# Layer 1's second memory-value group computed in layer 0's last norm, and that norm's modulation row summed by VectorE in layer 1's first feed forward

## The chip, the cores and the metric

The program runs on one core of one Trainium2 chip. The core has five engines that run their own instruction streams: TensorE (PE) for matmuls, VectorE (DVE) and ScalarE (ACT) for elementwise work, GpSimd (POOL), which here mostly issues gathers, and SyncE (SP), which here issues the weight loads. They meet only through semaphores. The metric is the device time of one execution in microseconds (us).

## What is computed

Two blocks run one after the other. The first (`first_block`) has two layers; each is a SwiGLU feed forward and a norm, a mixer (conv, recurrence, pooling) and a norm, cross attention to a memory `mem` and a norm, a second feed forward and a norm. The second block has two layers of attention and a product-key expert lookup (`peer_block`), modulated by rows that come from a condition vector. Cut to what the change touches:

```python
# first block, layer l
h = layer_norm(ALPHA * h + 0.5 * swiglu(h, ffn1_gate[l], ffn1_up[l], ffn1_down[l]), ln_g[l, 0], ln_b[l, 0])
z = h @ w_in[l]                                        # mixer input, 24 chunks of weights
...
h = layer_norm(ALPHA * h + mix, ln_g[l, 1], ln_b[l, 1])
v = (mem @ wv).reshape(bsz, m, CA_HEADS, CA_HEAD_DIM)   # depends on mem alone, not on h
o = jnp.einsum('bhsm,bmhd->bshd', p, v)                 # p: softmax of q k
h = layer_norm(ALPHA * h + cross_attn(...), ln_g[l, 2], ln_b[l, 2])
h = layer_norm(ALPHA * h + 0.5 * swiglu(h, ffn2_gate[l], ...), ln_g[l, 3], ln_b[l, 3])
# second block, layer i
mod = jax.nn.silu(c) @ ada_w[i] + ada_b[i]              # a "modulation row" is 512 of its 6144 columns
```

The activations `x` and `mem` have 256 tokens of 1024 features. Keys and values of the memory and the modulation rows depend on nothing that the first block computes, so they can be computed anywhere before their use.

## The kernel before, in words

Weights come in chunks of 512 KB. SP loads them in the order in which it is written, into two places. The feed forward's weights go into `fw`, two buffers for each of gate, up and down (`ff_loads`, L527 is the issue): the load of a tile waits until PE has used the tile two before it (`ff_done`). All other weights go through `wring`, four slots of one chunk (`load`, L510): each load waits until four chunks back has been used (`chunk_done`, one count that PE and DVE add to). SP issues in program order, so a load that stands behind another also starts behind it.

A feed forward is 22 tiles. For each, PE does 16 matmuls of gate and up (`gate_up`, L1529) and 8 of down (`down`, L1537), in the order gate_up(q+1), down(q). ACT makes the silu, DVE multiplies it with up (`hidden_tile`, L3148), and down(q) waits for that. DVE fills its time with expert work of the second block's context: per slot a gather of 512 KB by POOL (L712) into a ring of 8 (`rows`), and one instruction on DVE: a dot product (L2780) or a weighted sum (L2789). DVE does 8 of these (`HEAD_SLOTS`) behind hidden_tile(0), then 4 behind each hidden tile, in a loop of five turns of four tiles.

After a feed forward, PE, DVE and ACT pass the norm's work to and fro (`layer_norm`: residual L3249, mean L1568, centring L3258, squares on ACT, mean of squares L1568 again, reciprocal L3267, scaling L3271, x_t by ACT L1762). PE fills the waits with work that is given to it as `between`: in a layer's first norm the values of memory head 0 (`value_between`, L1592), in the second keys (`key_between`), in the third and fourth a modulation row (`mod_row_between`, which calls `mod_row_part`, L856: 8 matmuls of 512 columns). Further modulation rows are summed on DVE near the end of each feed forward (`mod_row_sums`, L3176 and L3179: 8 instructions over 512 columns, into `row_acc`), and PE only adds up the partitions with one matmul (L1560). ACT takes each row out of PSUM (`mod_row_take`, L1762) into the one buffer `mod_row` and writes it out by a small DMA (L1808), and waits at the next take until that DMA has landed.

In the mixer PE runs groups of two chunks (`group`; L787 and L796) and between them the levels of the recurrence (`level`, L1642), which DVE takes (`take_level`, L3358 and L3356). Behind level 8 stands group 13, memory head 1's values into `ca_v[:, 1]`, in both layers, and then PE waits for DVE's take of levels 7 and 8.

A matmul of 128x256 stands in the trace as two records, so "x32" is 16 matmuls.

Of the kernel before, what the change touches and what calls it, by code (L numbers as in the profile page):

```python
# [21 lines left out]
ALU = mybir.AluOpType  # L22
ACT = mybir.ActivationFunctionType
AX = mybir.AxisListType.X

P = 128
# [27 lines left out]
MIX_CHUNKS = 60  # L54
ADA_CHUNKS, QKV_CHUNKS, WO_CHUNKS, PQ_CHUNKS = 48, 12, 8, 16
# [156 lines left out]
def program(nc, a, out):  # L212

    with ExitStack() as ctx:
# [242 lines left out]
        row_acc = view(arena, 6656, 512)  # L457
        mod_tm = view(mem_tile, 7 * T, P)
# [28 lines left out]
        NORM_BANK = 3  # L487
# [16 lines left out]
        def _(eng):  # L504
# [37 lines left out]
            def mod_row_loads(i):  # L542
                chunk_loads(a["second_w"], LAYER_1 + WR * ROW_AT[i], WR)
# [17 lines left out]
            for l in range(L):  # L561
                mix_at, row_at = l * MIX_CHUNKS, CTX_MOD_ROWS + 4 * l
                for w in range(2):
# [3 lines left out]
                    if w == 0:  # L567
                        mod_row_loads(row_at)
# [4 lines left out]
                    with sp.loop(FT_TURNS, **ff_turn) as i:  # L573
# [3 lines left out]
                    if w == 0:  # L577
# [178 lines left out]
        def _(eng):  # L756
# [762 lines left out]
            def feed_forward(h_ready):  # L1519
# [25 lines left out]
                mod_row_free()  # L1545
                gate_up(1)
# [9 lines left out]
                pe.skip(chunk_done, WR)  # L1556
                for arrived in weights_in:
                    pe.skip(arrived, 16)
                eng.wait_ge(chunk_done, pe.now(chunk_done))
                mm(ps_d[0:2, :], mean_d[:, 0:2], row_acc, start=True, stop=True).then_inc(  # L1560
# [26 lines left out]
            def value_between(i0, i1):  # L1587
                for i in range(i0, i1):
                    b, k = i // KT, i % KT
                    if b == 0 and k % 4 == 0:  # L1590
                        chunk(k // 4)
                    ins = mm(ps_b[:, b * T:(b + 1) * T], mem_t[:, k, b * P:(b + 1) * P],  # L1592
# [25 lines left out]
            for l in range(L):  # L1618
                feed_forward(h_take if l else h_have)
                layer_norm(value_between)  # L1620

                def group(g, c, src, ready=None, tm=False, between=None):
                    eng.wait_ge(z_done, pe.now(z_done, 1))
                    odd = (g + 1 if g < 12 else g) % 2
                    bank = ps_b[:, odd * 512:(odd + 1) * 512]
                    if tm:
# [25 lines left out]
                group(13, 26, mem_t, tm=True)  # L1652
# [83 lines left out]
                layer_norm(mod_row_between, finish if l == L - 1 else None)  # L1736
# [21 lines left out]
        def _(eng):  # L1758
# [33 lines left out]
            def mod_row_take(i, bank, row):  # L1792

                if bank == 2:
# [1830 lines left out]
```

## Time and profile before

| | us |
|---|---|
| median of 3 runs | 3248.68 |
| lowest and highest | 3248.24, 3252.84 |
| the profiled execution | 3234.46 |
| its span on the core | 3232.2 |
| PE busy in the span | 3055.6 (95%) |
| DVE, ACT, POOL busy | 2133.4, 952.0, 1226.2 |
| layer 0's last norm (from the last down matmul to layer 1's first feed forward) | 964.66 to 976.20 |
| layer 1's first feed forward, on PE | 976.20 to 1206.09 |
| layer 1's first norm and mixer | 1206.09 to about 1370 |

Times inside the trace are from the span's start. A row of the timeline is: start, duration, engine, line, operation, how many records, and in brackets the idle time ahead of it with its releaser. PE's matmuls overlap by a little, so a stretch is best read from start to start.

### The profile page before, as it was taken

What the parts mean: (1) busy time and instruction counts of PE and PEld (TensorE: products, weight loads), DVE (VectorE), ACT (ScalarE), POOL (GpSimd) and SP (SyncE); (2) the same over time, 40 slices, a digit from 0 to 9 for tenths busy, and PEclk for the clock granted to TensorE, in tenths of its full rate; (3) what the DMA queues carried; (4) which work ended last, traced back from release to release, by engine and by line L of the source; (5) the groups of instructions that cost most, each with busy time, mean ns of one, the idle gap of its engine ahead of it and who ended that gap; (6) DMA issues with size and microseconds to landing.
All of it is one profiled execution on the core that took longest, in us unless ns stands there. A gap on an engine that the chain in (4) does not pass through costs nothing.

```text
span 3232.2 us, 39640 instructions
## 1 busy us (share of the span) xinstructions
PE 3055.6 (95%) x13179; PEld 2183.1 (68%) x13185; DVE 2133.4 (66%) x4328; ACT 952.0 (29%) x2504; POOL 1226.2 (38%) x1136
## 2 busy tenths in 40 slices
PE   9999999999999999999999999989888999987777
PEld 7688888888888888887885845535335855532224
DVE  7877889756555457766455695667555596577444
ACT  2320012211001002121003464335455464343333
POOL 1003545344435443343430254434443144444332
PEclk9999999999999999999999999999999999999999
DMA  9787989798998997788988899999999899999998
GB/s 363 256 288 281 373 352 350 267 359 330 355 353 347 356 330 272 268 338 344 354 308 294 336 422 419 421 419 421 418 421 378 319 420 420 421 421 421 421 421 352
DMA packets 252469, 1164.47 MB, mean 360 GB/s; under 512 B 27304, under 2 KB 34952, under 8 KB 186400
## 3 DMA queue, kind: packets, MB, share of 16 engines
q0 software_dynamic: 153792, 828.44, 63.6%
q1 hardware_dynamic: 98480, 334.10, 28.5%
q8 instruction: 80, 1.31, 0.2%
q14 instruction: 69, 0.57, 0.0%
q10 hardware_dynamic: 48, 0.05, 0.0%
HBM read 1161.39 MB, written 1.10 MB: 360 GB/s over the span
## 4 chain that ended last, share of the span: by engine, by line
PE 32%; DMA 16%; DVE 5%; ACT 4%; issue 1%; POOL 0%; ACTq 0%; SPq 0%; POOLq 0%; DVEq 0%
DMA ring<-in_peer_uv,idx 12%; PE ps_a L1471 12%; PE ps_b L1529 5%; DMA arena<-in_peer_uv,idx 3%; PE ps_a L1537 2%; DVE ring L2962 2%; ACT arena L1762 2%; PE ps_a L774 1%; PE ps_b L1292 1%; PE ps_b L1237 1%; PE ps_b L787 1%; ACT L1762 1%; PE ps_a L1292 1%; PE ps_b L1028 1%; ACT wts L1762 1%
## 5 line engine op out<-in xcount | busy, mean ns | idle before, releaser
L1471 PE MATMUL ps_a<-ring,arena 128*128 128x512 f32 x1728 | 819.4, 608 | 129.1 <-ACT arena L1762 128.6
L749 POOL DMA_INDIRECT ring<-in_peer_uv,idx x448 | 494.8, 1104 | 879.0 <-PE ps_a L1471 620.8
L2962 DVE SCALAR_TENSOR_TENSOR ring<-ring,h_tm 128x1024 f32<-128x1024 f32 x448 | 546.7, 1223 | 378.0 <-DMA ring<-in_peer_uv,idx 377.3
L712 POOL DMA_INDIRECT ring<-in_peer_uv,idx_now x512 | 580.7, 1134 | 415.3 <-DVE arena L2780 151.4
L1471 PEld LDWEIGHTS ps_a<-ring,arena 128*128 128x128 f32 x1728 | 308.1, 191 | 561.3 <-ACT arena L1762 293.8
L1529 PE MATMUL ps_b<-x_t,ring 128*128 128x256 f32 x2816 | 623.3, 380 | 0.8 <-DMA ring<-in_ffn 0.5
L1529 PEld LDWEIGHTS ps_b<-x_t,ring 128*128 128x128 f32 x2816 | 533.6, 190 | 79.0 <-ACT x_t L1762 3.5
L1762 ACT ACTIVATE arena<-ps_b 128x256 f32<-128x256 f32 (+3 forms) x218 | 99.3, 457 | 1195.9 <-PE ps_b L1529 827.7
L1537 PE MATMUL ps_a<-arena,ring 128*128 128x256 f32 x1408 | 318.7, 380 | 0.0
L2780 DVE SCALAR_TENSOR_TENSOR arena<-ring,h_tm 128x1024 f32<-128x1024 f32 x256 | 299.1, 1220 | 20.0 <-DMA ring<-in_peer_uv,idx_now 16.6
L1537 PEld LDWEIGHTS ps_a<-arena,ring 128*128 128x128 f32 x1408 | 267.7, 190 | 39.1 <-issue 3.5
L1762 ACT ACTIVATE wts<-dots 128x1 f32<-128x1 f32 (+1 forms) x514 | 103.8, 202 | 621.2 <-DVE ring L2962 529.1
L3148 DVE SCALAR_TENSOR_TENSOR arena<-ps_b,arena 128x256 f32<-128x256 f32 x88 | 37.3, 424 | 331.0 <-PE ps_b L1529 189.6
L1762 ACT ACTIVATE arena<-consts,wts 128x128 f32<-128x128 f32 x512 | 205.5, 401 | 52.9 <-PE ps_a L1471 5.0
L2789 DVE SCALAR_TENSOR_TENSOR arena<-ring,stage,arena 128x1024 f32<-128x1024 f32 x160 | 195.1, 1278 | 5.7 <-DMA ring<-in_peer_uv,idx_now 5.6
L787 PE MATMUL ps_b<-x_t,wring 128*128 128x256 f32 x896 | 197.8, 381 | 0.3
L787 PEld LDWEIGHTS ps_b<-x_t,wring 128*128 128x128 f32 x896 | 167.0, 190 | 27.6 <-ACT x_t L1762 4.6
L774 PE MATMUL ps_a<-arena,wring 128*128 128x256 f32 (+1 forms) x896 | 169.5, 350 | 3.1 <-ACT arena L1762 1.9
L774 PEld LDWEIGHTS ps_a<-arena,wring 128*128 128x128 f32 x896 | 150.6, 191 | 22.0 <-ACT arena L1762 2.7
L1762 ACT ACTIVATE wts<-wts,gates 128x1 f32<-128x1 f32 x512 | 150.7, 294 | 16.6
L2789 DVE SCALAR_TENSOR_TENSOR arena<-ring,wts,arena 128x1024 f32<-128x1024 f32 x92 | 114.9, 1288 | 50.6 <-DMA ring<-in_peer_uv,idx_now 50.4
L1762 ACT ACT_TABLE_LOAD x105 | 134.7, 1283 | 12.0 <-PE ps_b L1529 8.7
(460 smaller groups left out, 3357.9 us busy)
## 6 DMA issues: line engine op xcount, KB each, us to landing
ring<-in_ffn SPq DMA_DIRECT2D x264, 512.0 KB, 7.0
wring<-in_second_w SPq DMA_DIRECT2D x166, 512.0 KB, 4.8
wring<-in_mix_w SPq DMA_DIRECT2D x120, 512.0 KB, 6.4
ring<-in_ada_rows POOLq DMA_DIRECT2D x44, 512.0 KB, 5.7
ring<-in_second_w SPq DMA_DIRECT2D x12, 1024.0 KB, 10.2
ring<-in_peer_uv,idx_now POOLq DMA_INDIRECT x512, 8.4
ring<-in_peer_uv,idx POOLq DMA_INDIRECT x448, 14.8
arena<-in_second_w SPq DMA_DIRECT2D x13, 512.0 KB, 11.1
```

The lines of the kernel that those rows point to most:

```text
L712: G.indirect_dma_start(rows[:, s, :], None, table, bass.IndirectOffsetOnAxis(ap=idx_now[:, half, s:s + 1], axis=0)).then_inc(rows_in[s], p ...
L749: G.indirect_dma_start(pairs[slot].rearrange("p c d -> p (c d)"), None, a["peer_uv"], bass.IndirectOffsetOnAxis(ap=idx[:, b, s:s + 1], axi ...
L774: ins = mm(acc_t[:, j, cols], w[:, k * P:(k + 1) * P], src[:, k, cols], start=i == 0, stop=i == KT - 1)
L787: ins = mm(bank[:, t * T:(t + 1) * T], w[:, k * P:(k + 1) * P], src[:, k, :], start=k == 0, stop=k == KT - 1)
L1292: ins = mm(out, part_of(place, k), src[:, k, :], start=k == 0, stop=k == KT - 1)
L1471: ins = mm(ps_a[:, b * D + j * 512:b * D + (j + 1) * 512], diags[:, at % DIAGS, :], pairs[at % PAIRS][:, 1, j * 512:(j + 1) * 512], start= ...
L1529: ins = mm(bank[:, part * T:(part + 1) * T], fw[:, ft % 2, part, k * P:(k + 1) * P], x_t[:, k, :], start=k == 0, stop=k == KT - 1)
L1537: ins = mm(acc_t[:, j, :], fw[:, ft % 2, 2, j * P:(j + 1) * P], hidden[:, ft % 2, :], start=opens and j % 2 == 0, stop=last, skip_group_ch ...
L1762: return nc.scalar.activation(out, in_, func, **k)
L2780: V.scalar_tensor_tensor(acc[s % 2], rows[:, s, :], 1.0, h, ALU.mult, ALU.mult, accum_out=out).then_inc(row_used, ve.adds(row_used))
L2789: ins = V.scalar_tensor_tensor(acc[s % 2], rows[:, s, :], w, acc[s % 2], ALU.mult, ALU.add)
L2962: V.scalar_tensor_tensor(row, row, 1.0, h_tm[:, n // SLOTS, :], ALU.mult, ALU.mult, accum_out=dots[:, n % SLOTS:n % SLOTS + 1]).then_inc(d ...
```

## The change

Four things change. (1) Layer 0's last norm gets `moved_between` in place of `mod_row_between`: 16 matmuls that compute layer 1's head 1 values (chunks 26 and 27 of layer 1's mixer weights, constant `MOVED`) into PSUM bank 1; ACT evicts them to `moved_v`, a place of its own. (2) In layer 1's mixer group 13 is gone; the chunks and slots behind the first two move by two, and layer 1's first norm takes its values from slots 2 and 3. (3) The modulation row that stood in the norm (row index 6) is summed by DVE in layer 1's first feed forward, behind the 8 head slots and ahead of the loop, into `row_acc_2`; PE gets one more matmul at that feed forward's end, into `ps_c`, and ACT one more take there. (4) SP's loads follow: two chunks instead of four ahead of layer 1's feed forward, row 6's four chunks where row 7's stood, and row 7's four chunks between the fourth and the fifth turn of that feed forward's loop of loads.

```diff
+MOVED = 26
+        row_acc_2 = view(arena, 7168, 512)
+        moved_v = view(extra, 2 * D, NB, T)
...
                     if w == 0:
-                        mod_row_loads(row_at)
+                        mod_row_loads(row_at - l, 2 * l)
...
-                    with sp.loop(FT_TURNS, **ff_turn) as i:
+                    looped = FT_TURNS - 1 if (l, w) == (1, 0) else FT_TURNS
+                    with sp.loop(looped, **ff_turn) as i:
...
+                    elif (l, w) == (1, 0):
+                        mod_row_loads(row_at, 2)
+                        for ft in range(FT_STEP):
+                            for part in range(3):
+                                ff_loads(looped * FT_STEP + (l * (2 * FT) + (w * FT + 2 + ft)), ft, part)
+                        chunk_loads(a["mix_w"], mix_at, 2, 2)
+                        chunk_loads(a["mix_w"], mix_at + 2, MOVED - 2)
+                        chunk_loads(a["mix_w"], mix_at + MOVED + 2, MIX_CHUNKS - WR - MOVED - 2)
+                    elif l == 0:
+                        chunk_loads(a["mix_w"], MIX_CHUNKS + MOVED, 2)
...
                 gate_up(0, True)
                 mod_row_free()
+                if second_row:
+                    eng.wait_ge(z_done, pe.now(z_done))
                 gate_up(1)
...
+                if second_row:
+                    mm(ps_c[0:2, :], mean_d[:, 0:2], row_acc_2, start=True, stop=True).then_inc(
+                        row_summed, pe.adds(row_summed))
+                    pe.skip(mod_row_taken, 1)
                 mm(ps_d[0:2, :], mean_d[:, 0:2], row_acc, start=True, stop=True).then_inc(
...
                 between(0, 1)
+                if between == value_between and l:
+                    eng.wait_ge(mod_row_taken, pe.now(mod_row_taken, 1))
...
+            def moved_between(i0, i1):
+                if i0 == 0:
+                    mod_row_free()
+                for i in range(i0, i1):
+                    b, k = i // KT, i % KT
                     if b == 0 and k % 4 == 0:
                         chunk(k // 4)
+                    ins = mm(ps_b[:, 512 + b * T:512 + (b + 1) * T], mem_t[:, k, b * P:(b + 1) * P],
                              wring[:, k // 4, (k % 4) * T:(k % 4 + 1) * T], start=k == 0, stop=k == KT - 1)
...
-                group(13, 26, mem_t, tm=True)
+                if l == 0:
+                    group(13, MOVED, mem_t, tm=True)
...
-                                v = (ca_v0, ca_v[:, 1], early_v[l], ca_v[:, 3])[h][:, m, :]
+                                v = (ca_v0, moved_v if l else ca_v[:, 1], early_v[l], ca_v[:, 3])[h][:, m, :]
...
-                layer_norm(mod_row_between, finish if l == L - 1 else None)
+                layer_norm(mod_row_between if l else moved_between, finish if l == L - 1 else None)
...
                 feed_forward()
+                if l:
+                    mod_row_take(row_at - 1, SECOND_ROW, mod_row)
                 mod_row_take(row_at, 2, mod_row)
...
                 hidden_tile(0)
                 some_slots(summing, h, at, HEAD_SLOTS, acc_first)
+                if (l, w) == (1, 0):
+                    mod_row_sums(l, w, row_acc_2, 1)
                 with ve.loop(FT_TURNS, up_done=FT_STEP, silu_done=FT_STEP, down_done=FT_STEP, hidden_done=FT_STEP,
```

How the order of instructions moves, at the three places that matter. PE in layer 1's mixer, around level 8, before (L787 a group, L1642 levels, L796 the value group, L1658 to L1660 what needs the taken levels):

```order
212 L787 MATMUL ps_b<-x_t,wring 128x256 x16
213 L1642 MATMUL ps_a<-arena 128x128 x12
214 L796 MATMUL ps_b<-wring,mem_t 128x256 x16
215 L1658 MATMUL ps_a<-arena 128x128
216 L1659 MATMUL ps_a<-arena 128x128
217 L1660 MATMUL ps_a<-arena 128x128
```

and after the change (L801 is the group, L1682 the levels, L1699 to L1701 the rest):

```order
214 L801 MATMUL ps_b<-x_t,wring 128x256 x16
215 L1682 MATMUL ps_a<-arena 128x128 x12
216 L1699 MATMUL ps_a<-arena 128x128
217 L1700 MATMUL ps_a<-arena 128x128
218 L1701 MATMUL ps_a<-arena 128x128
```

The 16 matmuls of group 13 no longer stand between the levels and the work that waits for DVE's take of them.

DVE at the start of layer 1's first feed forward, before (L3148 is a hidden tile, L2780 the dot slots, the branch begins the loop):

```order
371 L3277 COPY vec_tile<-vec_tile 128x340
372 L3148 SCALAR_TENSOR_TENSOR arena<-ps_b,arena 128x256
373 L2780 SCALAR_TENSOR_TENSOR arena,dots<-ring,h_tm 128x1024 x8
374 L202 UNCONDITIONAL_BRANCH
375 L202 ISA
```

and after (L3230 and L3233 are the sum of the modulation row, L3200 the hidden tile):

```order
371 L3333 COPY vec_tile<-vec_tile 128x340
372 L3200 SCALAR_TENSOR_TENSOR arena<-ps_b,arena 128x256
373 L2832 SCALAR_TENSOR_TENSOR arena,dots<-ring,h_tm 128x1024 x8
374 L3230 TENSOR_SCALAR arena<-wring,cond 128x512
375 L3233 SCALAR_TENSOR_TENSOR arena<-wring,cond,arena 128x512 x7
376 L203 UNCONDITIONAL_BRANCH
377 L203 ISA
378 L3196 ISA
379 L3197 REGISTER_ALU
380 L3200 SCALAR_TENSOR_TENSOR arena<-ps_b,arena 128x256
```

Eight instructions now stand ahead of hidden_tile(1).

SP at the end of layer 1's first feed forward, before (the end of the loop of loads, then the loop of mixer chunks):

```order
172 L527 DMA ring<-in_ffn 128x1024
173 L527 ISA
174 L527 DMA ring<-in_ffn 128x1024
175 L202 REGISTER_ALU
176 L202 COMPARE_AND_BRANCH
177 L202 UNCONDITIONAL_BRANCH
178 L202 ISA
179 L510 ISA
180 L510 DMA wring<-in_mix_w 128x1024
```

and after:

```order
175 L203 REGISTER_ALU
176 L203 COMPARE_AND_BRANCH
177 L513 DMA wring<-in_second_w 128x1024 x4
178 L530 DMA ring<-in_ffn 128x1024 x12
179 L513 DMA wring<-in_mix_w 128x1024 x2
180 L203 UNCONDITIONAL_BRANCH
```

Four chunks of a modulation row now stand ahead of the loads of the last four tiles.

## Rows read from the trace of the kernel before

**Rows 1.** The page, engines: busy us, share of the span, instructions
```profile
PE 3055.6 (95%) x13179; PEld 2183.1 (68%) x13185; DVE 2133.4 (66%) x4328; ACT 952.0 (29%) x2504; POOL 1226.2 (38%) x1136
```

**Rows 2.** Busy times by stretch: us, PE, PEld, DVE, ACT, POOL, PEclk, DMA share, GB/s
```profile
965.00:1206.00 241.00, 240.63 (x1090) 204.03 (x1089) 130.00 (x234) 19.01 (x39) 111.28 (x99) 1.00 0.94 351
```

**Rows 3.** Timeline of PE, layer 1's mixer around group 13 (L796)
```profile
1313.39 2.84 PE L1642 MATMUL ps_a<-arena 128*128 128x128 f32 x24
1316.07 7.07 PE L796 MATMUL ps_b<-wring,mem_t 128*128 128x256 f32 x32
1322.98 0.38 PE L1658 MATMUL ps_a<-arena 128*128 128x128 f32 x2
```

**Rows 4.** Timeline of DVE in the same stretch
```profile
1316.72 0.68 DVE L3356 COPY arena<-ps_a 128x512 f32<-128x512 f32 x1
...
1325.66 0.69 DVE L3413 TENSOR_TENSOR arena<-arena 128x512 f32<-128x512 f32 x1
1332.17 6.55 DVE L3418 RECIPROCAL arena<-arena 128x1024 f32<-128x1024 f32 x1 [5.82 <-ACT arena L1762]
```

**Rows 5.** Timeline of PE, layer 0's last norm with its modulation row
```profile
960.15 1.02 PE L1560 MATMUL ps_d<-arena,consts 128*2 128x512 f32 x2
961.10 3.72 PE L1537 MATMUL ps_a<-arena,ring 128*128 128x256 f32 x16
964.66 1.18 PE L1568 MATMUL ps_c<-arena,consts 128*128 128x256 f32 x4
...
976.20 14.40 PE L1529 MATMUL ps_b<-x_t,ring 128*128 128x256 f32 x64
```

**Rows 6.** Timeline of PE, layer 1's first norm with a value group
```profile
1206.09 0.59 PE L1592 MATMUL ps_b<-wring,mem_t 128*128 128x256 f32 x2
...
1217.14 28.23 PE L787 MATMUL ps_b<-x_t,wring 128*128 128x256 f32 x128
```

**Rows 7.** Timeline of DVE, layer 1's first feed forward: hidden_tile(1); the row's sum at its end
```profile
995.05 0.42 DVE L3148 SCALAR_TENSOR_TENSOR arena<-ps_b,arena 128x256 f32<-128x256 f32 x1
...
1193.70 0.70 DVE L3176 TENSOR_SCALAR arena<-wring,cond 128x512 f32<-128x512 f32 x1
...
1200.11 0.41 DVE L3148 SCALAR_TENSOR_TENSOR arena<-ps_b,arena 128x256 f32<-128x256 f32 x1
```

**Rows 8.** Timeline of PE, the same feed forward: gate_up(2), down(1), gate_up(3)
```profile
993.89 7.07 PE L1529 MATMUL ps_b<-x_t,ring 128*128 128x256 f32 x32
1000.80 3.62 PE L1537 MATMUL ps_a<-arena,ring 128*128 128x256 f32 x16
1004.25 5.99 PE L1529 MATMUL ps_b<-x_t,ring 128*128 128x256 f32 x27
```

**Rows 9.** SP's waits (965:1206), and L527's time to landing in 1128:1165 and 1003:1036
```profile
SPq L527 <- PE ps_a L1537: 176.3, 21, 9.9
...
DMA to landing us min/median/max: 4.3/7.1/9.0
...
DMA to landing us min/median/max: 6.8/8.5/10.8
```

**Rows 10.** DMA traffic of 1120:1200, by queue (packets, MB, share of 16 engines), then of 1000:1040
```profile
q0 software_dynamic: 4564, 16.64, 53.9%
q1 hardware_dynamic: 3162, 11.51, 42.0%
...
DMA packets 4511, 16.43 MB, mean 411 GB/s; under 512 B 503, under 2 KB 503, under 8 KB 4510
```

**Rows 11.** Timeline of ACT, the take of a row and the squares of layer 1's first norm
```profile
1202.64 0.59 ACT L1762 ACTIVATE arena<-ps_d 2x512 f32<-2x512 f32 x1 [3.96 <-PE ps_d L1560]
1203.26 0.24 ACTq L1808 DMA_DIRECT2D mod_rows<-arena  x1
1209.40 2.42 ACT L1762 ACTIVATE arena<-arena 128x512 f32<-128x512 f32 x4 [6.17 <-DVE arena L3258]
```

**Rows 12.** DMA issues: out<-in, engine, count, size, us to landing
```profile
second<-in_vecs SPq DMA_DIRECT2D x1, 78.0 KB, 1.9
```

More of the change, by code:

```diff
@@ L486, in program @@
         Q_FREE, OWN_FREE = 3, SLOTS + 36
-        NORM_BANK = 3
+        NORM_BANK, SECOND_ROW = 3, 4
         KEPT_DMAS = [sum(len(place) for place in kept_places[l]) for l in range(L)]
@@ L540, in _, with mod_row_loads @@
             chunk_loads(a["early_w"], 6, 2, 2)
-            def mod_row_loads(i):
-                chunk_loads(a["second_w"], LAYER_1 + WR * ROW_AT[i], WR)
+            def mod_row_loads(i, first=0):
+                chunk_loads(a["second_w"], LAYER_1 + WR * ROW_AT[i], WR, first)
             chunk_loads(a["second_w"], FIRST_ADA, QKV_CHUNKS)
@@ L1623, in group @@
                     eng.wait_ge(z_done, pe.now(z_done, 1))
-                    odd = (g + 1 if g < 12 else g) % 2
+                    odd = (g + 1 if g < 12 or l and g < 18 else g) % 2
                     bank = ps_b[:, odd * 512:(odd + 1) * 512]
+                    if l and c < MOVED:
+                        c += 2
                     if tm:
@@ L1792, in mod_row_take @@
             def mod_row_take(i, bank, row):
-                if bank == 2:
+                if bank in (2, SECOND_ROW):
                     eng.wait_ge(row_summed, ac.next(row_summed))
@@ L2302, in group @@
                 def group(g, dst, func=ACT.Copy):
-                    odd = (g + 1 if g < 12 else g) % 2
+                    odd = (g + 1 if g < 12 or l and g < 18 else g) % 2
                     eng.wait_ge(chunk_done, ac.next(chunk_done, 2))
@@ L2328, in _ @@
                 group(11, z_g[:, 2:4, :], ACT.Sigmoid)
-                group(13, ca_v[:, 1])
+                if l == 0:
+                    group(13, ca_v[:, 1])
                 eng.wait_ge(o_done, ac.next(o_done))
@@ L2378, in _ @@
                 layer_norm(3)
-                mod_row_take(row_at + 3, 1, mod_row)
+                if l == 0:
+                    eng.wait_ge(chunk_done, ac.next(chunk_done, 2))
+                    act(moved_v, ps_b[:, 512:1024].rearrange("p (b t) -> p b t", t=T), ACT.Copy).then_inc(
+                        z_done, ac.adds(z_done))
+                else:
+                    mod_row_take(row_at + 3, 1, mod_row)
             for l in range(L):
@@ L3166, in later_search, with mod_row_sums @@
                     expert_ids(0, 1, 4, split=True)
-            def mod_row_sums(l, w):
-                loads = ROW_LOADS + l * (MIX_CHUNKS // WR + 4) + w * (MIX_CHUNKS // WR + 2)
+            def mod_row_sums(l, w, row=row_acc, back=0):
+                loads = ROW_LOADS + l * (MIX_CHUNKS // WR + 4) + w * (MIX_CHUNKS // WR + 2) - back
+                first = 2 if (l, w) == (1, 0) else 0
                 for k in range(KT):
-                    part, weight = wring[:, k // 2, k % 2 * 512:(k % 2 + 1) * 512], cond[:, 2 * k:2 * k + 1]
+                    s = (first + k // 2) % WR
+                    part, weight = wring[:, s, k % 2 * 512:(k % 2 + 1) * 512], cond[:, 2 * k:2 * k + 1]
                     if k % 2 == 0:
-                        eng.wait_ge(weights_in[k // 2], 16 * loads)
+                        eng.wait_ge(weights_in[s], 16 * (loads + 1 if s < first else loads))
                     if k == 0:
-                        ins = V.tensor_scalar(row_acc, part, weight, None, ALU.mult)
+                        ins = V.tensor_scalar(row, part, weight, None, ALU.mult)
                     else:
                         eng.wait_ge(row_step, ve.now(row_step))
-                        ins = V.scalar_tensor_tensor(row_acc, part, weight, row_acc, ALU.mult, ALU.add)
+                        ins = V.scalar_tensor_tensor(row, part, weight, row, ALU.mult, ALU.add)
                     if k < KT - 1:
@@ L3459, in _ @@
                 layer_norm()
-                ve.skip(chunk_done, WR)
+                if l == 0:
+                    ve.skip(chunk_done, 2)
+                    ve.skip(z_done, 1)
+                else:
+                    ve.skip(chunk_done, WR)
                 ve.skip(h_done, 4 * KT)
```

32 lines of the change are left out of this document (22 added, 10 removed).

## The prediction

> **What bounds the kernel now.** I read the engines' totals first: PE is busy 95% of the span, DVE 66% [rows 1]. An average over stages says little, so I read the stretch that the change touches next: from 965 to 1206 us PE is busy 240.63 of 241.00 us, DVE 130 us, at full granted clock, and the DMA engines are busy 94% of it at 351 GB/s [rows 2]. So through layer 0's last norm and layer 1's first feed forward PE is the bound. What PE no longer does there is saved, and what makes PE wait is lost, one for one; the second resource without much room is DMA, not DVE. Then I read the timelines of PE, DVE and ACT at each place that the diff touches, from the start of one group to the start of the next, since matmuls overlap. The sum is made against the profiled execution (3234.46 us, span 3232.2). The median of the runs is 3248.68, 14 us above it; I take the same difference in us for both and put the sum onto the median.
>
> **Group 13 leaves layer 1's mixer.** It takes PE from 1316.07 to 1322.98, 6.91 us [rows 3]. It covers something: the matmuls behind it wait until DVE has taken levels 7 and 8. That take ends at 1316.72 + 0.68 = 1317.40 [rows 4], 1.3 us after level 8 is through PE at 1316.07 [rows 3]. Without the group PE stands from 1316.07 to about 1317.5 (0.1 for the semaphore, my estimate), so 1.4 comes back as a new wait: gain 5.5, between 5.2 and 5.6. Who is late next? DVE's pooling work ends at 1325.66 + 0.69 = 1326.35 and does not move, since it hangs on the take, not on group 13; the reciprocal behind it now starts at 1332.17, released by ACT [rows 4]. With PE 5.5 earlier ACT releases it at about 1326.7, so DVE is just free: 0.3 us of cover is left. What follows on DVE (the output of the recurrence, 8 dot slots, and the gathers that their ring slots release) hangs on that reciprocal and moves along. ACT loses one eviction, which nobody waited for.
>
> **Layer 0's last norm.** With its modulation row it takes 964.66 to 976.20 on PE, 11.54 us [rows 5]. Layer 1's first norm has exactly the form that the changed one gets, one value matmul ahead of the mean, 7 between the means and 8 behind: 1206.09 to 1217.14, 11.05 us [rows 6]. Gain 0.5, between 0 and 0.6. The changed form starts with a matmul where PE now has nothing to do, and its fill is as long (16 matmuls against 8 that are twice as wide). Its ACT eviction stands where the row's take stood, and PE needs that bank only at gate_up(1), 7 us into the feed forward: nothing.
>
> **One more matmul at the end of the feed forward.** The one that is there takes 960.15 to 961.10, 0.95 us [rows 5]: cost 0.95. Its input has been ready for 200 us.
>
> **The sum on DVE.** The same 8 instructions at the feed forward's end take 1193.70 to 1200.11, 6.4 us [rows 7]. They now stand between the head slots and hidden_tile(1), which starts at 995.05 and takes 0.42 [rows 7]. So it ends at 995.05 + 6.4 + 0.42 = 1001.9. PE wants it at 1000.80, when gate_up(2) is through and down(1) can start [rows 8]. Queued behind the eight instructions are that hidden tile and every later slot, and PE waits for the tile: 1.1 plus 0.1 for the semaphore, cost 1.2, between 1.0 and 1.5. It is paid once, as later hidden tiles have room: DVE is busy 130 us of 241 [rows 2]. The slots behind it start late, but they were waiting for their gathers there.
>
> **The four chunks in SP's queue.** This is the term that decides. PE does a tile in 1004.25 - 993.89 = 10.36 us [rows 8]. SP waits 21 times for a down matmul [rows 9]: once per tile, at the end of down(q), it issues down(q+2), gate(q+3) and up(q+3) together, 1.57 MB, and gate(q+3) is wanted 10.36 us later. These loads land in 4.3 to 9.0 us in the late tiles, 6.8 to 10.8 where the gathers are behind [rows 9]. So a gate load now has some 3 us to spare. With the change, at the end of down(15) (1004.25 + 14 x 10.36, about 1149) four chunks go between down(17) and gate(18). Their slots of the ring were free long before, so all are issued at once, and gate(18) becomes the sixth load in line instead of the second, 3.15 MB instead of 1.05. From the first landing of three to the third it is (10.8 - 6.8) / 2 = 2.0 us per load in the crowded tiles, (9.0 - 4.3) / 2 = 2.35 in the late ones [rows 9]. Sixth in line: 4.3 + 5 x 2.35 = 16 us, or 6.8 + 5 x 2.0 = 17; with 0.7 us from the end of down to SP's first issue (my estimate) against 10.36 that is 6.4 to 7.2 us of waiting. From below: if the whole 411 GB/s that the engines reach when crowded [rows 10] went to SP's queue, 3.15 MB would take 7.7 us, plus about 2 to land (nearest row: 78 KB in 1.9 us [rows 12]), and PE would wait 0. Both queues are at work (16.64 MB of gathers against 11.51 MB of loads in 80 us [rows 10]), which is why I stay near the upper rows; but while PE stands, DVE gets no hidden tile, takes no slots and so asks for no gathers, which frees bandwidth exactly then. I take 5, from 0 to 8.
>
> The DMA engines serve gathers and loads at the same time [rows 10]. The Trainium skill (DMA: Bandwidth & Descriptors, section Queues, rings and completion order) says that each engine goes round robin between its queues, a packet at a time. By that SP's queue would have half while gathers wait, an estimate of 0.2 MB per us from 411 GB/s, 3.15 MB would take 15.3 us, and the wait would come to about 7; the sum would be 2 us higher than mine.
>
> **The second take on ACT.** Row 6's take comes first, row 7's must wait until the small DMA of the first has landed, since both use one buffer. Before: take at 1202.64, DMA at 1203.26, and ACT is next wanted at 1209.40 for the squares [rows 11]. The first take now stands where that one stands, the squares 0.95 later. Between issue and squares lie 7.1 us, minus 0.6 for the second take, so a landing within 6.5 costs nothing. No row shows how long 4 KB take to DRAM; the nearest are 1.9 us for 78 KB on an idle queue [rows 12] and up to 10.8 for 512 KB in the crowd [rows 9]. I take the small one: cost 0, at most 4.
>
> **Sum.** -5.5 - 0.5 + 0.95 + 1.2 + 5 + 0 = +1.15. Profiled execution about 3235.6; median 3248.68 + 1.15 = 3249.8.
>
> **Rivals.**
> *The burst is absorbed.* The ffn loads have room (SP waits 176 us of 241 for PE [rows 9]), and the engines can move 411 GB/s where they move 351 [rows 2, 10]. If gate(18) comes in time or within 1.5 us: -3.85 to -2.4, 3244.8 to 3246.3. Against it: 60 GB/s of room is 0.6 MB per tile, and 2.1 MB are added.
> *Slower.* The backlog lasts over two tiles. It decides from the point where SP's queue gets less than 0.2 MB per us: gate(18) then waits 7 to 8 us, and up(18) or gate(19), queued behind, another 3 to 5, since they were issued late as well. -3.85 + 11 = +7, 3255 to 3257. For it: with gathers behind, three loads already take up to 10.8 us [rows 9]. Against it: the pause in the gathers.
> *PE's arithmetic alone.* All waits are hidden, DVE's as well as the DMA's: -6.91 - 0.5 + 0.95 = -6.5, 3242.2. This needs the take of level 8 and hidden_tile(1) to come over 1 us earlier than the rows show; nothing in the profile is for it.
> *The change does not do what it says.* If layer 1's mixer were held by the gathers, not by PE, the 5.5 would be lost: +6.6, 3255.3. DVE finishes the slots ahead of the mixer's norm late, but they start from the dot slots that move along, so I give it little.
>
> **How the numbers follow.** Forecast (burst 2 to 7.5): 0.50, time 3246.8 to 3252.5. Burst absorbed: 0.26. Slower by the backlog: 0.09; gathers hold the mixer: 0.05. PE's arithmetic alone: 0.10. 0.2% is 6.5 us, about what a measurement of this kernel can tell from no change. Faster than that (below 3242.2) takes the last case and luck, 0.07 in all; slower (above 3255.2) most of the two slow cases, 0.11; the rest, 0.82, is within 0.2%. The range goes from 3243.0, just above the arithmetic case, to 3255.5, just into the slow ones, and leaves out some 0.18.
>
> **What would show it.** In the changed trace: PE goes from level 8 to L1699 with 1.4 us of idle time released by DVE; the last norm of layer 0 takes 11.0 us; down(1) of layer 1's first feed forward is preceded by about 1.2 us of waiting for DVE; gate_up(18), near 1159 us, by about 5 us of waiting for a DMA of in_ffn; the squares of the next norm start no later than 7.1 us behind the DMA of the first take. No wait at gate_up(18) would make the prediction wrong by its largest term; a wait in the mixer's norm for gathers would show the fourth rival.

## The result and the profile after

The changed kernel takes 3256.27 us (median of 15 runs, 3251.93 to 3263.38), the kernel before 3249.80 (15 runs beside it). The ratio is 1.0019, 95% interval 1.0012 to 1.0026: 6.2 us slower by the ratio, between 4 and 8. The forecast was 3249.8 with a range up to 3255.5, so the time fell outside, on the slow side, just short of the bound of 0.2%. In part that is the base: the kernel before measured 1.1 us more here than the 3248.68 that the forecast was added to. As a difference +6.2 to +6.5 stands against a forecast of +1.15 and an upper end of +6.8.

The profiled execution of the changed kernel takes 3256.03 us, that of before 3234.46. This difference of 22 us is not that of the medians, and it must not be explained as one: the first profile of before was 15 us under the median of its runs (the last section shows what it lacked). So I compare stretches, not spans. Two of them hold all that the change touches: stretch A from the row matmul that ends layer 0's second feed forward to the one that ends layer 1's first, and stretch B from there to the first mean of layer 1's mixer norm. A took 241.43 us before and takes 253.63 now, B 169.72 and 163.98. Together that is 12.2 - 5.7 = +6.5 us, as much as the difference of the medians.

The costliest groups of the page already say where: PE's gate and up matmuls wait for their weights, where they did not before (idle 0.8 there, 10.8 here).

```profile
L1543 PE MATMUL ps_b<-x_t,ring 128*128 128x256 f32 x2816 | 625.4, 381 | 10.8 <-DMA ring<-in_ffn 9.5
...
L1551 PE MATMUL ps_a<-arena,ring 128*128 128x256 f32 x1408 | 318.7, 379 | 0.9 <-DVE arena L3200 0.9
```

PE's timeline at tile 18 of layer 1's first feed forward (L1551 is down(16), then gate_up(18), down(17)):

```profile
1164.86 3.62 PE L1551 MATMUL ps_a<-arena,ring 128*128 128x256 f32 x16
1177.03 9.46 PE L1543 MATMUL ps_b<-x_t,ring 128*128 128x256 f32 x32 [8.56 <-DMA ring<-in_ffn]
1186.33 3.62 PE L1551 MATMUL ps_a<-arena,ring 128*128 128x256 f32 x16
```

From down to down it is 21.47 us in place of 10.36 [rows 8]: 11.1 us lost. 8.56 of them are waiting ahead of gate(18), 8.7 from start to start. The other 2.4 are inside the next row, which lasts 9.46 where a pair of gate and up lasts 7.07. They are no wait for up(18): PE has no gap in that row. They are PE's clock. The two parts of the row, with the window, its length, PE's busy time and number of records first, and the granted clock, the DMA share and GB/s last:

```profile
1177.03:1181.69 4.66, 4.66 (x11) 3.76 (x12) 0.00 (x0) 0.00 (x0) 0.00 (x0) 0.50 1.03 410
1181.69:1186.33 4.64, 4.64 (x23) 4.07 (x23) 0.00 (x0) 0.00 (x0) 0.00 (x0) 1.00 0.44 175
```

PE is busy through both. In the first part it gets through 11 records, in the second through 23 in the same time. PE had stood since 1168.5; the granted clock fell to 0.50 (1.2 GHz instead of 2.4) at 1171.5 and rose again at 1181.7, when PE had been back at work for 4.7 us.

The other places, PE again: layer 0's last norm, which answers to [rows 5], hidden_tile(1), the end of the feed forward, and the mixer, which answers to [rows 3].

```profile
972.69 0.59 PE L1630 MATMUL ps_b<-wring,mem_t 128*128 128x256 f32 x2
...
983.74 14.41 PE L1543 MATMUL ps_b<-x_t,ring 128*128 128x256 f32 x64
...
1001.44 7.07 PE L1543 MATMUL ps_b<-x_t,ring 128*128 128x256 f32 x32
1009.36 2.85 PE L1551 MATMUL ps_a<-arena,ring 128*128 128x256 f32 x12 [0.85 <-DVE arena L3200]
...
1220.95 1.02 PE L1578 MATMUL ps_c<-arena,consts 128*2 128x512 f32 x2
1221.81 1.02 PE L1581 MATMUL ps_d<-arena,consts 128*2 128x512 f32 x2
...
1333.30 2.84 PE L1682 MATMUL ps_a<-arena 128*128 128x128 f32 x24
1337.36 0.49 PE L1699 MATMUL ps_a<-arena 128*128 128x128 f32 x2 [1.22 <-DVE arena L3412]
```

The norm takes 983.74 - 972.69 = 11.05 us (11.54 before). down(1) starts 7.92 us after gate_up(2) where it was 6.91: 1.0 us. The added matmul costs 0.86. Level 8 to L1699 is 4.06 us; before it was 2.68 to group 13 and 6.91 for the group, 9.59 in all: gain 5.5.

ACT at the two takes, which answers to [rows 11]:

```profile
1222.63 0.24 ACTq L1852 DMA_DIRECT2D mod_rows<-arena  x1
1228.32 0.59 ACT L1803 ACTIVATE arena<-ps_d 2x512 f32<-2x512 f32 x1 [5.73 <-DMA mod_rows<-arena]
...
1229.63 2.42 ACT L1803 ACTIVATE arena<-arena 128x512 f32<-128x512 f32 x4 [0.72 <-DVE arena L3314]
```

The small DMA took 5.7 us to land. The second take ended 0.7 us before DVE released the squares: it cost nothing, but by a hair.

### The profile page after: what moved, and what is told of

The parts are those of the page before. It is cut to its first block, busy times and chain, and to the rows that moved or that the text cites. A ratio compares the mean times of both kernels' runs of the same rounds, so it can differ in the third digit from the quotient of the medians.

```text
span 3254.2 us, 39582 instructions
## 1 busy us (share of the span) xinstructions
PE 3057.9 (94%) x13165; PEld 2183.8 (67%) x13171; DVE 2138.1 (66%) x4336; ACT 951.5 (29%) x2504; POOL 1231.4 (38%) x1136
## 4 chain that ended last, share of the span: by engine, by line
PE 34%; DMA 13%; ACT 4%; DVE 4%; issue 2%; POOL 0%; another core or an unknown queue 0%; SPq 0%; ACTq 0%; POOLq 0%; DVEq 0%
PE ps_a L1485 14%; DMA ring<-in_peer_uv,idx 10%; PE ps_b L1543 4%; DMA arena<-in_peer_uv,idx 3%; ACT arena L1803 2%; PE ps_a L1551 2%; PE ps_a L788 2%; DVE ring L3014 2%; ACT L1803 1%; PE ps_b L1306 1%; PE ps_b L1251 1%; PE ps_a L1306 1%; PE ps_b L801 1%; PE ps_b L1042 1%; ACT wts L1803 1%
## 5 line engine op out<-in xcount | busy, mean ns | idle before, releaser
L1543 PE MATMUL ps_b<-x_t,ring 128*128 128x256 f32 x2816 | 625.4, 381 | 10.8 <-DMA ring<-in_ffn 9.5
L1551 PE MATMUL ps_a<-arena,ring 128*128 128x256 f32 x1408 | 318.7, 379 | 0.9 <-DVE arena L3200 0.9
L1551 PEld LDWEIGHTS ps_a<-arena,ring 128*128 128x128 f32 x1408 | 267.1, 190 | 40.8 <-issue 4.7
L3200 DVE SCALAR_TENSOR_TENSOR arena<-ps_b,arena 128x256 f32<-128x256 f32 x88 | 37.3, 424 | 350.4 <-PE ps_b L1543 184.2
L801 PE MATMUL ps_b<-x_t,wring 128*128 128x256 f32 x896 | 197.8, 381 | 0.3
L801 PEld LDWEIGHTS ps_b<-x_t,wring 128*128 128x128 f32 x896 | 166.7, 190 | 27.9 <-ACT x_t L1803 4.7
```

The source lines that it names most:

```text
L801: ins = mm(bank[:, t * T:(t + 1) * T], w[:, k * P:(k + 1) * P], src[:, k, :], start=k == 0, stop=k == KT - 1)
L1543: ins = mm(bank[:, part * T:(part + 1) * T], fw[:, ft % 2, part, k * P:(k + 1) * P], x_t[:, k, :], start=k == 0, stop=k == KT - 1)
L1551: ins = mm(acc_t[:, j, :], fw[:, ft % 2, 2, j * P:(j + 1) * P], hidden[:, ft % 2, :], start=opens and j % 2 == 0, stop=last, skip_group_ch ...
```

## Why 11 and not 5: the two queues share the engines, and a long wait costs clock

SP's issues and POOL's gathers around the wait, from the timelines of their queues:

```profile
1158.28 0.33 SPq L530 DMA_DIRECT2D ring<-in_ffn  x1
1158.82 2.77 SPq L513 DMA_DIRECT2D wring<-in_second_w  x4
1161.63 29.62 SPq L530 DMA_DIRECT2D ring<-in_ffn  x8
...
1172.96 0.94 POOL L726 DMA_INDIRECT ring<-in_peer_uv,idx_now  x1 [0.30 <-issue]
1189.31 1.14 POOL L726 DMA_INDIRECT ring<-in_peer_uv,idx_now  x1 [15.42 <-DVE arena L2832]
```

down(17), the four chunks of row 7, then gate(18): the order that was forecast. gate(18) was used 1177.03 - 1158.28 = 18.7 us after the first of the six loads was issued. The DMA traffic of 1158 to 1168 and of 1168 to 1184, by queue (packets, MB, share of the engines):

```profile
q1 hardware_dynamic: 482, 1.79, 49.6%
q0 software_dynamic: 479, 1.73, 45.7%
...
## 3 DMA queue, kind: packets, MB, share of 16 engines
q1 hardware_dynamic: 941, 3.40, 53.0%
q0 software_dynamic: 831, 3.02, 46.8%
```

SP's queue (q1) got 0.18 MB per us and then 0.21, the gathers (q0) 0.17 and 0.19, nearly as much. 3.15 MB at that rate are 16 to 17 us, and some 2 more make the 18.7. The Trainium skill (DMA: Bandwidth & Descriptors, section Queues, rings and completion order) has each engine take its queues in turn; the trace agrees, with halves of 1.79 and 1.73 MB.

Could 0.2 MB per us be all that SP's queue can do by itself? No. The kernel before, 965 to 975 us, where no gather is under way:

```profile
q1 hardware_dynamic: 1139, 4.15, 102.5%
```

That is 0.41 MB per us, for SP's queue alone. In the changed kernel too it rose, to 0.35, from 1172 to 1174, when the gathers had little under way, and it was back at 0.21 beside 0.20 for the gathers from 1174 to 1182. No run moved or left out the gathers, so the share is read from traces and not tested by an edit.

The gathers did not stop while PE stood (1168.5 to 1177.0). DVE had got hidden tile 17 before, had freed its slots, and POOL had issued four gathers between 1169 and 1173; it paused only then, for 15.42 us, and what was in flight went on at half of the engines' rate until 1184, 7 us after PE's wait had ended.

## The experiments

Theory A: the four chunks in SP's queue cost the 11 us, by their bytes, at half of the engines' rate. It does not count the clock, and puts 2 to 3 us on up(18) that are not there. The rivals are named with each run. The runs of this section stand in three groups, each on one chip; the kernel before took 3250.46, 3250.89 and 3237.34 us in them, so only the ratios compare across groups. Each profile gives stretches A and B, of one execution:

| kernel | A, us | B, us | PE's waits for weights in A, us (tile) | ratio to before, 95% |
|---|---|---|---|---|
| before | 241.43 | 169.72 | none | |
| before_again | 241.30 | 169.64 | none | |
| changed | 253.63 | 163.98 | 8.56 (18), and 2.4 by the clock | 1.0019 (1.0012 to 1.0026) |
| before_burst (the burst alone) | 251.11 | 170.54 | 7.66 (18), and 1.6 by the clock | 1.0032 (1.0020 to 1.0045) |
| pairs (two and two) | 247.27 | 163.92 | 2.06 (18), 2.17 (19) | 1.0008 (0.9999 to 1.0017) |
| after_thin (a quarter of the bytes) | 247.14 | 164.03 | 0.89 (4), 3.19 (18) | 1.0004 (0.9993 to 1.0015) |
| spread (one per tile) | 243.79 | 164.05 | 0.83 (18) | 0.9994 (0.9985 to 1.0003) |
| spread_again (the same) | 244.37 | 164.07 | 1.38 (18) | 0.9996 (0.9987 to 1.0005) |
| spread_split (DVE's sum in halves) | 244.03 | 163.97 | 0.42 (4), 0.40 (18), 0.98 (20) | 0.9995 (0.9986 to 1.0004) |
| sparse (one per second tile) | 246.75 | 165.66 | 0.42 (4), 2.09 (14), 0.92 (20) | 0.9995 (0.9986 to 1.0004) |
| no_row6 (group 13's move alone) | 242.15 | 164.08 | 0.48 (4) | 0.9993 (0.9983 to 1.0003) |

The granted clock is 1.00 through all of A except in the two kernels with the burst. Two cautions. The profiled execution was its kernel's fastest for pairs (3246.85 us, median 3253.93), no_row6 and spread_again, and the slowest for before_burst and sparse (3239.44, median 3235.18), so the waits of these are less sure for an ordinary run. And 0.4 to 0.9 us of waiting at tile 4 stand in four of the eight profiles that have group 13 moved, and in neither of the kernel before; nobody forecast them, and their cause is open.

### The burst alone, in the kernel before

```diff
                     if w == 0:
-                        mod_row_loads(row_at)
+                        if l == 0:
+                            mod_row_loads(row_at)
...
-                    with sp.loop(FT_TURNS, **ff_turn) as i:
+                    looped = FT_TURNS - 1 if (l, w) == (1, 0) else FT_TURNS
+                    with sp.loop(looped, **ff_turn) as i:
...
+                    if (l, w) == (1, 0):
+                        mod_row_loads(row_at)
+                        for ft in range(FT_STEP):
+                            for part in range(3):
+                                ff_loads(looped * FT_STEP + (l * (2 * FT) + (w * FT + 2 + ft)), ft, part)
```

> Edit: the kernel before, with one part of the change alone: row 7's four chunks are loaded between turns 4 and 5 of the loop of loads in layer 1's first feed forward, not ahead of it. Everything else as before, all of the output computed. Theory A (the four chunks in SP's queue cost PE 11 us, since SP's queue gets half of the DMA engines' 0.41 MB per us while gathers are under way): PE waits 8 to 9 us ahead of gate(18) and 2 to 3 ahead of up(18), 11 in all, and the time is 9 to 12 us over the kernel before. Theory B (the wait belongs to the changed kernel as a whole, to the later gathers behind the sum on DVE): the burst alone makes PE wait 3 us or less, and the time is within 3 us of the kernel before.

Measured: 3262.77 us against 3250.46, ratio 1.0032 (1.0020 to 1.0045), some 10 us slower by the ratio and 12 by the medians. PE at tile 18, and the first part of its middle row:

```profile
1166.56 3.62 PE L1544 MATMUL ps_a<-arena,ring 128*128 128x256 f32 x16
1177.83 8.68 PE L1536 MATMUL ps_b<-x_t,ring 128*128 128x256 f32 x32 [7.66 <-DMA ring<-in_ffn]
1186.35 3.62 PE L1544 MATMUL ps_a<-arena,ring 128*128 128x256 f32 x16
...
1177.83:1180.91 3.08, 3.08 (x7) 2.50 (x8) 0.00 (x0) 0.00 (x0) 0.00 (x0) 0.50 1.03 411
```

Almost the same loss at the same tile, 19.79 - 10.36 = 9.4 us, with nothing else of the change in the kernel. Theory B, that the wait belongs to the changed kernel as a whole, falls. SP's order of loads alone makes 9.4 of the 11.1 us; why the changed kernel loses 1.7 more is open. The wait ahead of gate(18), 7.66, is a little under the 8 to 9 expected, and the 2 to 3 ahead of up(18) were a miss: PE has no gap there, and the 1.6 us by which the row is longer come with the clock at 0.50 again.

### One chunk per tile

```diff
-                        mod_row_loads(row_at, 2)
                         for ft in range(FT_STEP):
+                            chunk_loads(a["second_w"], LAYER_1 + WR * ROW_AT[row_at] + ft, 1, (2 + ft) % WR)
                             for part in range(3):
                                 ff_loads(looped * FT_STEP + (l * (2 * FT) + (w * FT + 2 + ft)), ft, part)
```

> Edit: the changed kernel, with row 7's four chunks loaded one ahead of each of the last four tiles instead of all four ahead of the first of them. All of the output computed. Theory A: gate is third in line at each tile, not sixth; 1.57 MB at 0.2 MB per us and about 2 us to land are 10 us after the end of down, just in time, so PE waits 0 to 1 us per tile where it waited 11. Sum -5.6 (group 13) -0.5 (norm) +0.9 (matmul) +1.0 (hidden_tile(1)) + 0 to 2: 2 to 4 us under the kernel before, 8 to 11 under the changed one. Rival C (each added load costs 2 us or more wherever it stands, since the DMA engines are full): 4 waits of 2 us or more, no faster than the kernel before.

Measured: 3247.81 us against 3250.46, ratio 0.9994 (0.9985 to 1.0003). PE waits for weights once in A:

```profile
1173.49 7.17 PE L1543 MATMUL ps_b<-x_t,ring 128*128 128x256 f32 x32 [0.83 <-DMA ring<-in_ffn]
```

The bytes and the number of loads are those of the changed kernel; only their places in the queue differ, and the 11 us become 0.8. The clock stays at 1.00. In its profile A is 2.4 us longer than before and B 5.7 shorter: 3.3 us better. The median says 2.6 better. That is the direction that was expected, but the interval holds 1.

### Two and two

```diff
-                        mod_row_loads(row_at, 2)
                         for ft in range(FT_STEP):
+                            if ft < 2:
+                                chunk_loads(a["second_w"], LAYER_1 + WR * ROW_AT[row_at] + 2 * ft, 2, (2 + 2 * ft) % WR)
                             for part in range(3):
```

> Edit: the changed kernel, with row 7's chunks loaded two ahead of tile 18 and two ahead of tile 19. All of the output computed. Theory A: gate(18) is fourth in line, 2.1 MB at 0.2 MB per us plus 2 to land and 0.7 to issue are 13.2 us against 10.36: 2.8 us of waiting there, and about as much at gate(19) or a little less, since the line is already longer; 3 to 6 us in all, so 0 to 3 us over the kernel before. Rival C: the same 8 us or more as with four single loads.

Measured: 3253.93 us, ratio 1.0008 (0.9999 to 1.0017). PE's two waits:

```profile
1169.87 7.17 PE L1544 MATMUL ps_b<-x_t,ring 128*128 128x256 f32 x32 [2.06 <-DMA ring<-in_ffn]
1182.66 7.17 PE L1544 MATMUL ps_b<-x_t,ring 128*128 128x256 f32 x32 [2.17 <-DMA ring<-in_ffn]
```

4.2 us in all, in the expected 3 to 6, though in the fastest of its executions. So the cost of chunks ahead of a tile is not proportional: one costs 0.8, two 2.1, four 8.6 and then 2.4 of clock. The first is paid from the 3 us that a gate load has to spare; each further one adds some 2.6 us, 0.52 MB at 0.2 MB per us, by estimate, and the three measured waits follow that within 1.3 us.

### The same four loads, a quarter of the bytes

```diff
-                        mod_row_loads(row_at, 2)
+                        for j in range(WR):
+                            s = (2 + j) % WR
+                            eng.wait_ge(chunk_done, sp.next(chunk_done))
+                            eng.dma_start(wring[:, s, 0:256], a["second_w"][LAYER_1 + WR * ROW_AT[row_at] + j][:, 0:256]).then_inc(
+                                weights_in[s], sp.adds(weights_in[s], 16))
```

> Edit: the changed kernel, with row 7's four loads in the same place of SP's queue, but each of 256 of the 1024 columns, 128 KB instead of 512 KB. The other columns keep row 6's weights, so row 7 comes out wrong; no instruction of PE, DVE or ACT changes. Theory A (bytes at half the engines' rate): 1.57 MB less in line, 7.9 us less at 0.2 MB per us; of the 11 us of waiting at tile 18 0 to 3 remain, and the time is 2 to 5 us under the kernel before. Theory E (each load in line costs about 2 us whatever its size): the 11 us stay, and the time is 5 to 8 us over the kernel before.

Measured: 3249.63 us against 3250.89; ratio 1.0004 (0.9993 to 1.0015). PE at tile 18 (the profile attributes no landing to the loads of this run, so the wait is written to "issue"):

```profile
1174.17 7.17 PE L1547 MATMUL ps_b<-x_t,ring 128*128 128x256 f32 x32 [3.19 <-issue]
```

The 11.1 us became 3.2. That is 7.9 us less, the very number of theory A, but by accident: 2.4 of them are the clock, which stays at 1.00 here. The wait ahead of gate(18) itself went from 8.56 to 3.19, 5.4 us, where 1.57 MB at 0.2 MB per us are 7.9. Theory E, under which the wait stays as it was, falls, and the bytes are the larger part. But the bytes ahead of gate(18) are now those of spread and spread_again, which waited 0.83 and 1.38, so some 2 us come from something else in these loads: that there are three more of them, or that each moves rows of a quarter of the length. No run separates the two. The 3.19 are a little over the 0 to 3 expected, and the time was a miss: 2 to 5 us under the kernel before was expected, and the ratio says 1.3 over, from 2.3 under to 4.9 over.

### Group 13's move alone

The four loads and the eight instructions of row 6 are left out, row 7 is loaded where the kernel before has it:

```diff
-                        mod_row_loads(row_at - l, 2 * l)
+                        mod_row_loads(row_at, 2 * l)
...
-                    looped = FT_TURNS - 1 if (l, w) == (1, 0) else FT_TURNS
+                    looped = FT_TURNS
...
-                        mod_row_loads(row_at, 2)
...
-                    mm(ps_c[0:2, :], mean_d[:, 0:2], row_acc_2, start=True, stop=True).then_inc(
+                    mm(ps_c[0:2, :], mean_d[:, 0:2], row_acc, start=True, stop=True).then_inc(
...
-                if (l, w) == (1, 0):
-                    mod_row_sums(l, w, row_acc_2, 1)
```

> Edit: the changed kernel with the modulation row of layer 0's last norm left out: its four chunks are not loaded and not summed on DVE, row 7 is loaded where the kernel before loads it, and the second matmul and take at the end of the feed forward work on row 7 again. Row 6 therefore is wrong. What is left is the move of group 13 alone. Theory A: no wait at hidden_tile(1) and none for in_ffn, -5.6 -0.5 +0.9, 5 us under the kernel before (ratio 0.9984). Rival F (group 13's removal is given back later in the mixer, at the norm that waits for the gathers): 0 to 2 us under the kernel before.

Measured: 3248.15 us against 3250.89, ratio 0.9993 (0.9983 to 1.0003): 2.3 us better, with the expected 5 just inside the interval and no change inside as well. In the profile A is 0.7 longer and B 5.6 shorter, 4.9 better, and B ends at the norm that rival F named. So the gain is not given back there; the runs alone don't separate the two. Theory A had no wait for in_ffn, and there are 0.48 us at tile 4.

### Half of DVE's sum ahead of hidden_tile(0)

```diff
...
+                if (l, w) == (1, 0):
+                    mod_row_sums(l, w, row_acc_2, 1, 0, KT // 2)
                 hidden_tile(0)
                 some_slots(summing, h, at, HEAD_SLOTS, acc_first)
                 if (l, w) == (1, 0):
-                    mod_row_sums(l, w, row_acc_2, 1)
+                    mod_row_sums(l, w, row_acc_2, 1, KT // 2, KT)
```

> Edit: the kernel of spread, and the first four of the eight instructions of row 6's sum on DVE stand ahead of hidden_tile(0), where DVE is idle for 5.7 us, the other four where all eight stood. All of the output computed. Theory A: DVE reaches hidden_tile(1) 3.2 us earlier, ahead of PE's down(1); the wait of 0.85 to 1.0 us there goes, and the time is 1 us under spread. Rival D: the first half waits for its weights (slots 2 and 3 were loaded long before, so it should not) and hidden_tile(0) comes late: 0 to 3 us over spread.

Measured: 3248.95 us, ratio 0.9995 (0.9986 to 1.0004), no different from spread; the microsecond that was expected did not show. In the profile the wait for DVE at down(1) is gone, and PE waits for weights instead, three times:

```profile
1020.88 7.17 PE L1543 MATMUL ps_b<-x_t,ring 128*128 128x256 f32 x32 [0.42 <-DMA ring<-in_ffn]
1166.62 7.17 PE L1543 MATMUL ps_b<-x_t,ring 128*128 128x256 f32 x32 [0.40 <-DMA ring<-in_ffn]
1188.59 7.17 PE L1543 MATMUL ps_b<-x_t,ring 128*128 128x256 f32 x32 [0.98 <-DMA ring<-in_ffn]
```

A stays at 244.0. Whether the microsecond at down(1) would have been saved without those waits isn't settled by one profile.

### One chunk ahead of every second tile

```diff
-                    looped = FT_TURNS - 1 if (l, w) == (1, 0) else FT_TURNS
+                    looped = FT_TURNS - 2 if (l, w) == (1, 0) else FT_TURNS
...
-                        mod_row_loads(row_at, 2)
-                        for ft in range(FT_STEP):
+                        for ft in range(2 * FT_STEP):
+                            if ft % 2 == 0:
+                                chunk_loads(a["second_w"], LAYER_1 + WR * ROW_AT[row_at] + ft // 2, 1, (2 + ft // 2) % WR)
```

> Edit: the changed kernel, with row 7's four chunks loaded one ahead of every second of the last eight tiles (14, 16, 18, 20). All of the output computed. Theory A: a gate load third in line just makes its time, and with a tile between two added chunks the line is empty again before the next; no wait for in_ffn at these tiles, so the stretch from the row matmul of layer 0's second feed forward to that of layer 1's first (241.4 us before, 243.8 in spread) is 243.0, and the time is 2 to 6 us under the kernel before. Rival C: each added chunk costs a wait of its own wherever it stands: the stretch is 244 us or more.

Measured: 3235.18 us against 3237.34, ratio 0.9995 (0.9986 to 1.0004). The expectation for stretch A was a miss: 246.75 us where 243.0 was forecast, with 2.09 us of waiting at tile 14 and 0.92 at tile 20, and B is 1.6 us longer than in the other kernels with the move, by a wait at the norm that ends it:

```profile
1123.90 7.17 PE L1544 MATMUL ps_b<-x_t,ring 128*128 128x256 f32 x32 [2.09 <-DMA ring<-in_ffn]
1187.25 7.17 PE L1544 MATMUL ps_b<-x_t,ring 128*128 128x256 f32 x32 [0.92 <-DMA ring<-in_ffn]
...
1374.68 0.70 PE L1590 MATMUL ps_c<-arena,consts 128*128 128x256 f32 x2 [1.56 <-DVE arena L3296]
```

A single chunk costs between 0 and 2 us; what decides it is not shown. More room between the chunks doesn't make it free. In the last row DVE is late behind slots that waited for their gathers six times between 1356 and 1372, 9.7 us in all (some 8 us in the changed kernel, where PE does not wait). That is the sign by which the prediction would have known its fourth rival, here for 1.6 of the 5.5 us. This execution was the slowest of eleven, 4.3 us over their median, so none of it need be in the ordinary run. The kernel of spread ran beside it:

> The kernel of spread once more, beside sparse on the same chip, for its distance from the kernel before: 1 to 5 us under it, and within 1.5 us of sparse.

Measured: 3235.00 us against 3237.34, ratio 0.9996 (0.9987 to 1.0005), equal to sparse. Two groups of runs on two chips put spread 1.3 to 2 us under the kernel before by their ratios, 2.3 to 2.6 by their medians, and each interval alone holds 1. No other version that computes all of the output is clearly better; that spread beats the kernel before is likely and not shown.

## Why the prediction was wrong, by its own steps

**Group 13 leaves the mixer: right.** 5.5 forecast, 5.5 at the place, 5.7 over stretch B. The named new wait is there, 1.22 us for DVE's take (1.4 forecast), and the reciprocal starts with 0.40 us to spare instead of 5.82 [rows 4]. Both the changed kernel and no_row6 have the gain still whole at the norm that ends B, so the fourth rival is out for them. It is near: one execution of sparse lost 1.6 us there.

**The last norm: right.** 0.5 forecast, 0.49.

**One more matmul: right.** 0.95 forecast, 0.86.

**The sum on DVE: right.** 1.2 forecast, 1.0 with 0.85 of it marked as a wait for DVE.

**The second take: right by luck, with 0.7 us to spare.** The landing took 5.7 us, not the 1.9 of the row on which the cost of 0 rested; only the bound of 6.5 held.

**The four chunks: the term that was mis-sized.** Forecast 5, measured 11.1, and 9.4 with the burst alone. The place, the tile and the wait behind the added loads were right; three steps of the arithmetic were not. First, a spacing of 2.0 to 2.35 us per load was taken for six loads, which gave 16 to 17 us from the first issue; it was 18.7. The spacing came from the smallest and the largest landing in a window of several tiles [rows 9], not from the three loads of one tile. The rate that counts is half of the engines', 0.2 MB per us. The prediction had it in a sentence beside the sum and did not use it: 15.3 us for the bytes and a wait of 7, or 7.6 with the 2 us to land and the 0.7 to issue of the sum itself, which is still short of 8.6. Second, 1.4 to 2.2 us were taken off because gathers would pause while PE stands. The wait was over at 1177, and those already issued went on until 1184. Third, the wait was counted and what it does to PE's clock was put at nothing: the granted clock went to 0.50 while PE stood, and the first 4.7 us of work behind the wait ran at it, for 2.4 us more. With these, 8.7 + 2.4 in place of 5, the sum is +7.2, and the medians gave +6.5.

The slower rival had the total (+7) and half of its reason. Its 7 to 8 us for gate(18) were near the 8.6, and its condition, SP's queue at less than 0.2 MB per us, was met in the first 10 us (0.18) and just missed in the 16 behind them (0.21). Its other 3 to 5 us, a wait of up(18) or gate(19), did not come; the clock's 2.4 stood in for them, so that the sum came out is luck. The first half should have been the forecast: the profile had gathers and loads together through the whole stretch [rows 10], and the discount against it rested on no row.

## What to carry to other kernels

A load that is put into a queue of loads is paid by the load behind it, and beside a busy second queue at a smaller rate than the engines' full one: here 0.2 MB per us beside the gathers and 0.41 alone. Find the slack of the load behind (here 3 us) and divide the added bytes by the shared rate. Four chunks placed one at a time cost 0.8 to 3 us in all in these profiles, and in one piece 11. A stalled consumer does not free the bandwidth at once, since what its partners have issued still runs. And a long wait of PE costs more than its length: behind the waits of 7.7 and 8.6 us the granted clock was 0.50 and the work took 1.6 and 2.4 us longer, while in stretch A of all other kernels it stayed at 1.00. So look at the granted clock before a longer row behind a wait is called a second wait.

## What the runs showed that was not expected

A write of 4 KB to DRAM took 5.7 us to land, while SP's queue moved 1.71 MB in 7 us (1222 to 1229).

PE has waits in cross attention that come and go from execution to execution. The kernel before, profiled once more, PE and then ACT in layer 0:

```profile
696.63 1.16 PE L1715 MATMUL ps_b<-arena,extra 128*128 128x128 f32 x8 [1.91 <-issue]
...
701.04 29.55 PE L774 MATMUL ps_a<-arena,wring 128*128 128x256 f32 x128 [2.36 <-ACT arena L1762]
...
695.98 0.60 ACT L1762 ACTIVATE arena<-ps_b 128x512 f32<-128x512 f32 x1 [4.19 <-PE ps_b L1715]
700.30 1.09 ACT L1762 ACTIVATE arena<-ps_b 128x512 f32<-128x512 f32 x2 [3.72 <-remote]
```

> The kernel before, unchanged, profiled once more. Its first profiled execution was 15 us under the median of its runs and has no wait of PE at the output of cross attention (L1715), where all the other profiles have one of 1.9 to 2.0 us in both layers. If these waits belong to the kernel's ordinary runs, they stand here too and the span is 3240 us or more; if they belong to the change or to a shift of the code, this profile is like the first, near 3232.

Measured: 3246.78 us in one run, span 3244.5, with the waits in both layers. From one mean to the next across layer 1's cross attention (the mixer norm's first mean to the next norm's) it took 97.0 us here and 98.0 in the changed kernel, but 90.9 in the first profile of before, 90.0 in spread_again and 90.4 in no_row6. So they come with neither kernel, and they make some 6 to 7 us in layer 1. The clock has a part in it: in before_again PE takes 29.3 us from L774 behind the waits to the next mean, where the first profile of before takes 27.6, and its first 3.3 us have the clock at 0.50:

```profile
1445.93:1449.19 3.26, 3.26 (x8) 2.61 (x9) 1.45 (x2) 0.34 (x1) 1.67 (x3) 0.50 1.03 410
```

The waits explain why the first profile of before was faster than its runs, and why stretches had to be compared instead of spans. Both profiles of the last group, spread_again and sparse, are without them at L1715's place, which may be why the kernel before took 13 us less there; there is no profile of it from that chip. What starts the waits, the profiles don't say: PE's are marked "issue" for the most part, and one of ACT's "remote", a source that the profile doesn't know. It stays open.
